# Reading weight tiles by pairs of columns from their two halves, with the splits kept in order

## The reference

```
h = x + (softmax(q k' + cum_i - cum_j) v) @ fox_w_out        # q, k, v, f from rms_norm(x) @ fox_w_in
up = rms_norm(h) @ ffn_w_up;  y = causal_conv3(up)
h = h + (silu(gate(y)) * val(y)) @ ffn_w_down
z = rms_norm(h) @ w_in_2                                    # 2048 x 11264
h = h + (gate_a * (hgrn2(z) @ w_branch_a) + gate_b * (band_attention(z) @ w_branch_b)) @ w_out_2
h = h + square(relu(rms_norm(h) @ w_up_2)) @ w_down_2;  return rms_norm(h)
```

## Time and profile before

| what | value |
|---|---|
| median of 3 runs | 2482.05 us (2477.94 to 2483.34) |
| time of the profiled execution | 2480.14 us |
| its span | 2478.3 us |
| mean granted TensorE clock | 0.994 |
| PE matmul busy | 2424.9 us, 98% |
| PE weight load busy | 2117.6 us, 85% |
| DVE (VectorE) busy | 1883.7 us, 76% |
| ACT (ScalarE) busy | 1709.0 us, 69% |
| POOL (GpSimd) busy | 223.2 us, 9% |
| DMA | 545.79 MB, 220 GB/s on average |

### The profile page before, as it was taken

How to read it: one execution, slowest core, us unless ns; L and a number is a source line. 1 busy time by engine, 2 the same in 40 slices (tenths; PEclk the granted TensorE clock), 3 DMA queues, 4 the chain that set the end, 5 groups by cost and what they waited for, 6 DMA issues and landing times. The chain is left out here.

```text
span 2478.3 us, 32506 instructions
## 1 busy us (share of the span) xinstructions
PE 2424.9 (98%) x11468; PEld 2117.6 (85%) x11468; DVE 1883.7 (76%) x1831; ACT 1709.0 (69%) x1617; POOL 223.2 (9%) x365
## 2 busy tenths in 40 slices
PE   8999999999999999999999999999999999999997
PEld 7888888888888888887988888888888888888886
DVE  6677767888888888886888666577677777777776
ACT  7666668877777777775465667776766666666665
POOL 0122201100000000000010100000110000000000
PEclk9999999999999999999999999999999999999999
DMA  7877768887788788756566767677777777777775
GB/s 228 262 210 214 207 181 252 246 237 238 235 237 236 236 236 235 215 179 204 184 198 188 237 179 214 176 221 239 245 231 226 230 227 227 227 227 229 231 225 160
DMA packets 270391, 545.79 MB, mean 220 GB/s; under 512 B 22011, under 2 KB 23395, under 8 KB 270179
## 3 DMA queue, kind: packets, MB, share of 16 engines
q1 hardware_dynamic: 244064, 469.82, 62.6%
q0 software_dynamic: 22192, 70.28, 10.1%
q10 hardware_dynamic: 4051, 4.59, 0.6%
HBM read 508.93 MB, written 35.68 MB: 220 GB/s over the span
## 5 line engine op out<-in xcount | busy, mean ns | idle before, releaser
L897 ACT ACTIVATE w_hi<-raw 128x1024 fp32r<-128x1024 f32 x887 | 1373.8, 1567 | 547.9 <-PE acc L498 385.8
L1408 DVE TENSOR_TENSOR w_lo<-raw,w_hi 128x1024 fp32r<-128x1024 f32 x887 | 1327.0, 1508 | 496.4 <-ACT w_hi L897 490.3
L496 PE MATMUL acc<-w_hi,A_hi 128*128 128x512 f32 x1932 | 743.6, 385 | 6.1 <-ACT scratch L910 3.5
L497 PE MATMUL acc<-w_lo,A_hi 128*128 128x512 f32 x1932 | 733.1, 379 | 0.0
L498 PE MATMUL acc<-w_hi,A_lo 128*128 128x512 f32 x1932 | 732.9, 379 | 0.0
L496 PEld LDWEIGHTS acc<-w_hi,A_hi 128*128 128x128 f32 x1932 | 365.9, 189 | 59.8 <-DVE w_lo L1408 4.6
L498 PEld LDWEIGHTS acc<-w_hi,A_lo 128*128 128x128 f32 x1932 | 365.9, 189 | 51.6
L497 PEld LDWEIGHTS acc<-w_lo,A_hi 128*128 128x128 f32 x1932 | 366.0, 189 | 50.0
L496 PE MATMUL acc<-w_hi,C_hi 128*128 128x512 f32 x800 | 305.2, 381 | 6.3 <-DVE resid L1455 4.6
L496 PE MATMUL acc<-w_hi,B_hi 128*128 128x512 f32 x800 | 305.7, 382 | 3.1 <-DVE w_lo L1408 2.2
L497 PE MATMUL acc<-w_lo,C_hi 128*128 128x512 f32 x800 | 304.5, 381 | 0.0
(11 more groups left out here) (208 smaller groups left out, 1312.3 us busy)
## 6 DMA issues: line engine op xcount, KB each, us to landing
raw<-in_up SPq DMA_DIRECT2D x304, 512.0 KB, 4.5
raw<-in_w SPq DMA_DIRECT2D x271, 512.0 KB, 4.5
raw<-in_down SPq DMA_DIRECT2D x216, 512.0 KB, 4.8
raw<-in_wo SPq DMA_DIRECT2D x64, 512.0 KB, 5.2
turn_rows<-scratch POOLq DMA_DIRECT2D x23, 512.0 KB, 3.1
scratch<-turn_rows POOLq DMA_DIRECT2D x92, 128.0 KB, 5.2
up_rows<-scratch POOLq DMA_DIRECT2D x21, 512.0 KB, 4.8
scratch<-up_rows POOLq DMA_DIRECT2D x84, 128.0 KB, 5.6
```

Of the source, the lines that this page charges most:

```text
L496: pe.matmul(o, hi[:, kt, ts], wh, start=first and kk == 0, stop=False)
L497: pe.matmul(o, hi[:, kt, ts], wl, start=False, stop=False)
L897: act.activation(by_half(w_hi[:, q % RING, :]), even_odd(raw[:, q % RING, :]), ACT.Copy).then_inc(w_hi_ready, 1)
L1408: dve.tensor_tensor(by_half(w_lo[:, q % RING, :]), even_odd(raw[:, q % RING, :]), f32(by_half(w_hi[:, q % RING, :])), ALU.subtract).then_i ...
```

## The change

The splits no longer reorder columns: `w_hi` and `w_lo` are written in natural order from `raw` read in natural order, in contiguous accesses. The three helper views `even_odd`, `by_half` and `columns` are gone. `in_turn` is now a view with three steps and is used for the weight tile and for the output bank alike: two neighbouring columns of the first half (8 bytes), two of the second half, the next two of the first, and so on. TensorE so reads the columns in the order 0, 1, 256, 257, 2, 3, 258, 259, ... and writes each to the place of the same number in the bank, so that the bank is in natural order when it is full. The number of instructions on each engine, their order, their waits, the loads and all readers of the banks stay as they are.

```
-        def even_odd(v):
-            return v.rearrange("p (k n h) -> p k h n", n=CW // 2, h=2)
-        def by_half(v):
-            return v.rearrange("p (k h n) -> p k h n", n=CW // 2, h=2)
-        def in_turn(w):
-            return w.rearrange("p (h n) -> p n h", h=2)
-        def columns(o):
-            return o.rearrange("p (n h) -> p n h", h=2)
+        def in_turn(v):
+            return v.rearrange("p (h n q) -> p n h q", h=2, q=2)
 # gemm; the same in gemm_first and last_downs
                         wh, wl = (in_turn(w[:, ring, kk * CW:(kk + 1) * CW]) for w in (w_hi, w_lo))
-                        o, ts = columns(acc[:, banks[t], :]), slice(t * P, (t + 1) * P)
+                        o, ts = in_turn(acc[:, banks[t], :]), slice(t * P, (t + 1) * P)
 # split on ScalarE; the same for one tile in early_split
-                act.activation(by_half(w_hi[:, q % RING, :]), even_odd(raw[:, q % RING, :]), ACT.Copy).then_inc(w_hi_ready, 1)
+                act.activation(w_hi[:, q % RING, :], raw[:, q % RING, :], ACT.Copy).then_inc(w_hi_ready, 1)
 # split on VectorE; the same for one tile in early_split
-                dve.tensor_tensor(by_half(w_lo[:, q % RING, :]), even_odd(raw[:, q % RING, :]),
-                                  f32(by_half(w_hi[:, q % RING, :])), ALU.subtract).then_inc(w_lo_ready, 1)
+                dve.tensor_tensor(w_lo[:, q % RING, :], raw[:, q % RING, :], f32(w_hi[:, q % RING, :]),
+                                  ALU.subtract).then_inc(w_lo_ready, 1)
```

More of the change, by code:

```diff
@@ L538, in gemm_first @@
                     wh, wl = (in_turn(w[:, 0, kk * CW:(kk + 1) * CW]) for w in (w_hi, w_lo))
-                    o = [columns(acc[:, b, :]) for b in BK[0]]
+                    o = [in_turn(acc[:, b, :]) for b in BK[0]]
                     for t in range(TT):
@@ L873, in last_downs @@
                             pe.wait_ge(w_lo_ready, RING * (R_END - 2) + q + 1)
-                        o, ts = columns(acc[:, D2_LAST[q // 2][t], :]), slice(t * P, (t + 1) * P)
+                        o, ts = in_turn(acc[:, D2_LAST[q // 2][t], :]), slice(t * P, (t + 1) * P)
                         for kk in range(SLOT_K):
@@ L975, in early_split @@
                 v = slice(kk * CW, (kk + 1) * CW)
-                return act.activation(by_half(w_hi[:, 0, v]), even_odd(raw[:, 0, v]), ACT.Copy)
+                return act.activation(w_hi[:, 0, v], raw[:, 0, v], ACT.Copy)
             act.wait_ge(w_early, 16)
@@ L1490, in early_split @@
                 dve.wait_ge((w0_hi, w_hi_ready)[kk], 1)
-                return dve.tensor_tensor(by_half(w_lo[:, 0, v]), even_odd(raw[:, 0, v]), f32(by_half(w_hi[:, 0, v])), ALU.subtract)
+                return dve.tensor_tensor(w_lo[:, 0, v], raw[:, 0, v], f32(w_hi[:, 0, v]), ALU.subtract)
             early_split(0).then_inc(w0_lo, 1)
```

## The result

The changed kernel takes 3698.35 us (3698.25 to 3698.70, 4 runs) against 2482.7 us of the kernel before on the same chip: 1.4901 times as long, with a 95% interval of 1.4875 to 1.4926. The forecast of 2468 us and the range of 2450 to 2600 us both fail.

What follows compares the result with a forecast made beforehand. TensorE's products were taken to bound the kernel. From 2480.1 us, 13.9 us came off for faster splits and nothing was added for read or write: 2466.2 us, 2468 us as median, range 2450 to 2600 us.

Steps and rivals of the forecast that it cites:

- What bounds the kernel: TensorE's 10,644 products at 0.2159 us make 2298 of 2478.3 us; 1 ns per product is worth 10.6 us.
- The splits' durations: Splits beside busy TensorE fall to contiguous copies' times: ScalarE 1590 to 1048 ns, VectorE 1529 to 1214 ns.
- The bound "nothing, if the contention comes from TensorE's way of reading": Lower bound on the splits' gain: no gain if TensorE's reading slows the contiguous splits as well.
- Their share in the end: Faster splits shorten TensorE's inner waits: 13.9 us less, taken as 14, with bounds of 0 and 31.7 us.
- The read of the weight tile: TensorE's read by pairs costs nothing extra; bounds 0 to 11.2 ns per product, up to +119 us.
- the range's upper end: 2600 us, taking in the weight-tile read's whole bound and leaving out the bank write's.
- The write of the bank: TensorE's write by pairs at two places costs nothing; upper bound +56 to +112 ns per product, +596 to +1192 us.
- the second: Rival, slower by the weight-tile read: 2528 us with half of the 11.2 ns, 2587 us with the whole; chance 0.18.
- The third: Rival, slower by the bank write in two places: 3078 to 3674 us; chance 0.20.
- my sign for it, a step of 270 ns or more: In the profile after, a step between products of 270 ns or more would point to the bank write.
- The Trainium skill's rule on reads: Two successive hits on a 16-byte line for full speed would make the changed read faster; no gain taken.

Runs made afterwards that it cites:

- experiment 7: Splits in three forms on ScalarE and VectorE, TensorE idle or reading in three ways, nothing computed: ScalarE's strided form took 1563 ns beside single-column alternation, 1116 beside contiguous reads.
- experiment 5: Kernel before with only the splits put in order, TensorE still alternating single columns, so output columns permuted: 2442.83 us, ratio 0.9840.
- experiment 10: TensorE alone, numbers of stationary and moving columns varied, nothing computed: contiguous read 119 to 120 ns at 256 columns, 227 at 512; pairs 168 and 335 ns.
- experiments 2 and 3: Changed kernel with the weight tile read contiguously: bank still written by pairs (2), 2549.45 us; bank written contiguously too (3), 2549.96 us.
- experiment 8: TensorE alone, only the read's order varied (distances, parts, runs, bf16), contiguous writes, nothing computed: alternation by one 216 ns at distances of 4 to 256 columns.
- experiment 4: TensorE alone, 21 sections of 48 products with different reads and writes, nothing computed: contiguous read 226 ns, by one 215, by pairs (line 93) 340.

## Why the prediction was wrong

- What bounds the kernel: right. 1 ns per product was said to be worth 10.6 us; 117 ns more made 1250 us.
- The splits' durations: right, 1061 and 1224 ns against 1048 and 1214 forecast, though the copies that they were taken from read in runs of 32 columns and not in one line. The reading of the earlier trace rows was wrong in one half: only VectorE's split ran while TensorE stood idle. ScalarE's, 310.36 to 311.48 us, ran almost wholly beside products of line 604 that read in order. That it took 1.12 us was a first sign of what experiment 7 shows. The bound "nothing, if the contention comes from TensorE's way of reading" had the cause half right: it does come from the alternation, but only strided splits feel it.
- Their share in the end: the mechanism right, the term too small, 39 us alone and not 14. I counted only the waits that the view of waits lists, each with one split, and nothing for stalls inside PE's busy time. And I read the clock as full from 40 slices of 62 us each, in which three stretches of 3.4 to 6.8 us at 0.50 do not show; they were worth some 5 us (experiment 5).
- The read of the weight tile: this is the step that failed. "No product of the trace reads in pairs, so its cost has to be bounded by its two neighbours": 216 ns on one side, 227 on the other. Both neighbours were right to the nanosecond, and the value said to lie between them is 333: the term that I put at nothing measured 117 ns a product, 1250 us. Pairs are not between singles and a contiguous read in what they cost, only in how they look. I took 0 within those bounds; the range's upper end rested on the same sentence. That 227 came out was itself luck: I doubled an excess of 5.6 ns because the columns double, and by experiment 10 the excess of a contiguous read does not go with the columns.
- The write of the bank: the forecast of nothing is right, in the whole kernel (experiments 2 and 3) and in all run lengths alone. The Trainium skill (Advanced Engine Details and Errata, section PSUM Cachelines) says that any pattern that isn't contiguous slows matmuls significantly; the 2549.45 against 2549.96 us do not agree. Its next sentence, that pairs should be contiguous, agrees, though writes in steps of one were not tried.
- The rivals: the second had the right place and at most 119 of 1230 us. The third came near the measured time, 3078 to 3674 us, for a reason that is shown to be wrong, and my sign for it, a step of 270 ns or more, would have blamed the write for what the read did. A number that fits is no evidence for its story.
- The Trainium skill's rule on reads (Advanced Engine Details and Errata, section SBUF Cachelines) asks for at least two hits on a line of 16 bytes. I took no gain from it, and for fp32r the runs do not agree with it: pairs have two hits and take 340 ns, singles have none and are the fastest at 216. In bf16 the order of singles (484 ns) and contiguous (216 ns) is the rule's, though pairs took 271 there.

What stays open is the mechanism of the read. Shown is that it lies in TensorE's moving read alone, that it grows by the column, and that it depends on the start within 16 bytes. Two readers taking turns would give the order of some patterns but neither of all nor their sizes. Nor is it known why the read by pairs takes 340 ns in some sections and 329 in another (experiment 8: 168.3 to 178.5 us, 31 steps).

## What to carry to other kernels

An access order for which no row of the trace exists has no upper bound from orders that look similar; a section of 48 such matmuls took 16 us on the chip (experiment 4, line 93) and would have settled this one. If a stage stands on TensorE's step, weigh each change of a moving read in nanoseconds times products before anything on another engine. Where an engine pair pays for an order of columns, look for the one that pays nothing: here readers of PSUM.

## What the hardware showed unexpectedly

- A moving read of 512 fp32r columns, others idle: alternating single columns of two lines 215 ns, contiguous 226, fours 251, four parts in turn 281, pairs 340, even columns first 453. In bf16 alternation costs 484 and contiguous 216.
- Writing a PSUM bank in runs of 2 to 128 columns at two places costs TensorE nothing (226 to 228 ns), and neither does reading it in steps of two cost VectorE (1216 ns). Writes in single columns were not measured.
- ScalarE's copy of 1024 columns in steps of two takes 1121 ns alone, 1563 ns beside TensorE's alternation, 1163 ns beside its read by pairs.
- A write alternating between two halves costs ScalarE 1968 ns against 1045 in order, with TensorE idle.
